# Rotation tables built by GpSimd during the networks ahead, norm sums taken in the networks' last pass, final norm and store in one block

## The chip, the cores and the metric

The kernel runs on one core of one Trainium2 chip. The metric is device time in microseconds (us): the median of several runs, and beside it one profiled execution, whose trace all rows of this text are from. PE is TensorE's matmul stream and PEld its weight loads, DVE is VectorE, ACT is ScalarE, POOL is GpSimd, SP issues DMAs. Less is better.

## What is computed

Two models in a chain over 512 real tokens and 16 meta tokens, 1024 wide, all in float32. Each feed-forward network is a norm, a gated product and a residual:

```python
def _swiglu(x, wi, wo):
    a, b = jnp.split(x @ wi, 2, axis=-1)
    return (jax.nn.silu(a) * b) @ wo
h = h + 0.5 * _swiglu(_rms_norm(h, ln), wi, wo)
```

Six of them stand around three mixers: differential attention (8 heads), sparse latent attention (16 heads, top 128 keys), and a layer of three gated branches: a state-space scan, dilated attention and memory attention. The output is `rmsnorm(h, final_norm)`. The scan is a complex linear recurrence per state:

```python
dt = exp(log_dt); mag = exp(a_re * dt); ang = a_im * dt
abar = mag * (cos(ang) + i sin(ang))
coef = (abar - 1) / (a_re + i a_im)
x_t = abar * x_{t-1} + (coef * b) u_t          # 32 groups x 64 states, 512 steps
y_t = Re(c x_t) + d u_t
```

## The kernel before

The residual stream `h` lies in SBUF, transposed: 8 chunks of 128 channels by 528 tokens. The program is a row of stages, each one or more blocks in which all engines run their own streams and meet at the end. The order is `fa_` (network 0), `a_` (differential attention), `fb_` (networks 1 and 2), `bl_` and `l_` (latent attention), `fd_` (networks 3 and 4), `s_` (scan), `d_` (heads), `g_` (merge), `ff_` (network 5), `fin_` (final norm) and `out_` (store).

**A network** (`ffn_stage`) streams its weights through two slots. ScalarE rounds them to fp32r (`wh`), VectorE takes the rest (`wl`), and TensorE multiplies three times: high by high, high by low, low by high. The upward pass has 22 chunks. The downward pass has 8, one for each chunk of `h`; VectorE adds each result to `h` (L592, semaphore `dn_h`). Where a second network follows in the same stage, ScalarE squares each finished chunk (`square`), VectorE sums the squares in `ssum` (`add_square`), and one product with a matrix of ones gives the sum over channels. After the last network of a stage nothing of this happens. GpSimd only arms the next stage's semaphores.

**A stage's norm** starts in the stage itself. ScalarE squares the even chunks and VectorE the odd ones (in `fin_` ScalarE all), TensorE adds each by a product with ones, ScalarE takes the root, VectorE the reciprocal, and then it scales eight chunks. In `a_` each scaled chunk is also split in two parts, the rest by VectorE for even chunks and by GpSimd for odd ones, and GpSimd takes the rest of the weights (`split_weights`).

**The scan stage** (`scan_stage`) turns the complex recurrence into two real ones: the inputs are rotated by minus the accumulated angle, scanned with `mag`, and rotated back. There are 16 steps (`SC`), each with 128 states. VectorE first works out dt, mag and the angle from small tiles of 128x16 (`exact_exp`, ScalarE's two sines), raises the phase by squaring nine times (`phase`), and then makes `coef`, `bbar` and `b_wide`. GpSimd waits for all phases (`phased`), builds by doubling a `fine` table of 32 angles and a `coarse` one of 16 for each state, and multiplies them out to `turns` of 512 for each step, three deep. `turns` lies in `w`, which holds u's weights, so GpSimd also waits for `u_mm`. TensorE projects u (L1878), runs 3 of 24 gate projections (L1887, `EARLY = 3`), transposes `b_wide` (L1897) and `c_wide` (L1907), makes the inputs of steps 0 and 1 (L1917), and then loops:

```python
for s in range(SC):
    for n in at_step[s]:
        gate(n)
    pe.wait_ge(scanned, 1 + s + 1)
    ...                      # y of step s (L1932), two products
    if s + 2 < SC:
        inputs(s + 2)
```

`at_step` spreads the remaining gates evenly over the steps. A gate's weights come in a ring of three and its result goes to DRAM.

**The end**: `norm_stage` writes `y_out`, and in a block of its own SP stores it in one DMA of 2 MB.

## Time and profile before

| | us |
|---|---|
| median of 3 runs (3787.04 to 3789.86) | 3788.11 |
| the profiled execution | 3787.12 |
| its span in the trace | 3785.4 |
| TensorE busy | 3596.4 (95%) |
| VectorE busy | 1742.6 (46%) |
| ScalarE busy | 1297.5 (34%) |
| GpSimd busy | 354.2 (9%) |
| scan stage, from its first square to the last y's start | 2707.2 to 3004.1 |

Busy time is time in which the profiler saw an instruction of the engine. A 512-column float32 product with 128 rows counts as two matmul instructions, which overlap, so a row's time per instruction is longer than its share. The granted clock is TensorE's, 1.00 for 2.4 GHz and 0.50 for 1.2 GHz. The trace's mean is 0.974.

### The profile page before, as it was taken

The page shows a single profiled execution, that of the slowest core. Times are in us where ns is not written, and L with a number is a line of the kernel's source. Part 1 is how long each engine was busy: PE and PEld are TensorE (multiplying, and loading weights), DVE is VectorE, ACT ScalarE, POOL GpSimd, SP SyncE. Part 2 cuts the span into 40 slices and gives each one's busy share as a digit, 9 for nine tenths or more (in the row PEclk, how much of TensorE's full clock was granted, in tenths as well). Part 3 has the DMA queues.
Part 4 walks back from the last instruction along what each step waited for, and adds up shares of the span by engine and source line. Part 5 has one row for each costly group of instructions (what it writes and reads, how often), then busy time and mean ns, then how long its engine had stood idle before and what let it go on. Part 6 is the DMA issues. An engine that isn't in the chain of part 4 may idle for free. (4 is left out here: it accounts for less than half of the span.)

```text
span 3785.4 us, 50482 instructions
## 1 busy us (share of the span) xinstructions
PE 3596.4 (95%) x20176; PEld 2938.8 (78%) x20176; DVE 1742.6 (46%) x2620; ACT 1297.5 (34%) x1784; POOL 354.2 (9%) x263
## 2 busy tenths in 40 slices
PE   8999799799999999988999999999989899899998
PEld 7999777699999999754548888888634477678886
DVE  4442366444434443276625434443358633545432
ACT  4331266443323331134524423432110144324421
POOL 0000222100000000010000000000065333320000
PEclk9999899899999999989999999999989999899999
DMA  4322311022222222300013222222212321332221
GB/s 168 138 79 87 121 51 51 17 91 91 86 84 104 89 82 84 119 28 20 1 54 109 92 91 98 100 100 84 83 50 84 113 79 55 110 113 100 100 85 70
DMA packets 115306, 318.02 MB, mean 84 GB/s; under 512 B 13335, under 2 KB 56471, under 8 KB 99060
## 3 DMA queue, kind: packets, MB, share of 16 engines
q1 hardware_dynamic: 115188, 316.48, 24.6%
q8 instruction: 70, 1.15, 0.1%
q14 instruction: 48, 0.39, 0.0%
HBM read 307.95 MB, written 17.01 MB: 86 GB/s over the span
## 5 line engine op out<-in xcount | busy, mean ns | idle before, releaser
L368 PE MATMUL acc<-fb_xh,fb_wh 128*128 128x264 f32 x1408 | 287.9, 286 | 5.7 <-DVE fb_wl L518 5.7
L368 PE MATMUL acc<-fb_xl,fb_wh 128*128 128x264 f32 x1408 | 288.3, 286 | 0.0
L368 PE MATMUL acc<-fb_xh,fb_wl 128*128 128x264 f32 x1408 | 287.9, 286 | 0.0
L368 PE MATMUL acc<-fd_xh,fd_wh 128*128 128x512 f32 x704 | 275.7, 392 | 5.7 <-DVE fd_wl L518 5.7
L368 PE MATMUL acc<-fd_xl,fd_wh 128*128 128x512 f32 x704 | 274.7, 390 | 0.0
L368 PE MATMUL acc<-fd_xh,fd_wl 128*128 128x512 f32 x704 | 274.7, 390 | 0.0
L368 PEld LDWEIGHTS acc<-fb_xh,fb_wh 128*128 128x128 f32 x1408 | 220.2, 189 | 6.0 <-DVE fb_wl L518 5.9
L439 ACT ACTIVATE fb_wh<-fb_raw 128x2048 fp32r<-128x2048 f32 (+1 forms) x74 | 124.7, 1686 | 290.1 <-PE acc L427 176.9
L368 PEld LDWEIGHTS acc<-fb_xl,fb_wh 128*128 128x128 f32 x1408 | 219.4, 189 | 0.0
L368 PEld LDWEIGHTS acc<-fb_xh,fb_wl 128*128 128x128 f32 x1408 | 219.1, 189 | 0.0
L513 DVE TENSOR_TENSOR fb_wl<-fb_raw,fb_wh 128x2048 fp32r<-128x2048 f32 (+1 forms) x74 | 148.3, 2004 | 141.3 <-ACT fb_wh L439 140.5
L439 ACT ACTIVATE fd_wh<-fd_raw 128x2048 fp32r<-128x2048 f32 (+1 forms) x74 | 124.8, 1686 | 255.8 <-PE acc L427 162.4
L513 DVE TENSOR_TENSOR fd_wl<-fd_raw,fd_wh 128x2048 fp32r<-128x2048 f32 (+1 forms) x74 | 148.3, 2004 | 136.5 <-ACT fd_wh L439 135.5
L439 ACT ACT_TABLE_LOAD x60 | 77.0, 1283 | 301.2 <-PE acc L368 301.1
L1887 PE MATMUL acc<-m_xn,s_gw 128*128 128x512 f32 x384 | 171.4, 603 | 0.0
L368 PEld LDWEIGHTS acc<-fd_xh,fd_wh 128*128 128x128 f32 x704 | 132.7, 189 | 34.5 <-DVE fd_wl L518 6.5
L368 PEld LDWEIGHTS acc<-fd_xl,fd_wh 128*128 128x128 f32 x704 | 132.6, 188 | 27.9 <-issue 0.5
L368 PEld LDWEIGHTS acc<-fd_xh,fd_wl 128*128 128x128 f32 x704 | 132.6, 188 | 27.5
L368 PE MATMUL acc<-fa_xh,fa_wh 128*128 128x264 f32 x704 | 144.7, 287 | 9.3 <-DVE fa_wl L518 9.3
L592 DVE SCALAR_TENSOR_TENSOR h<-acc,h 128x264 f32<-128x264 f32 (+1 forms) x72 | 35.2, 516 | 254.0 <-PE acc L427 254.0
L1887 PEld LDWEIGHTS acc<-m_xn,s_gw 128*128 128x128 f32 x384 | 72.6, 192 | 98.1 <-issue 98.1
L368 PE MATMUL acc<-fa_xl,fa_wh 128*128 128x264 f32 x704 | 144.7, 287 | 0.0
(541 smaller groups left out, 8653.7 us busy)
## 6 DMA issues: line engine op xcount, KB each, us to landing
fb_raw<-wi_dram SPq DMA_DIRECT2D x42, 1024.0 KB, 4.8
fd_raw<-wi_dram SPq DMA_DIRECT2D x42, 1024.0 KB, 4.8
fb_raw<-wo_dram SPq DMA_DIRECT2D x32, 704.0 KB, 4.0
fd_raw<-wo_dram SPq DMA_DIRECT2D x32, 704.0 KB, 4.0
fa_raw<-wi_dram SPq DMA_DIRECT2D x20, 1024.0 KB, 4.8
ff_raw<-wi_dram SPq DMA_DIRECT2D x20, 1024.0 KB, 4.7
a_raw<-a_qkv_dram SPq DMA_DIRECT2D x24, 512.0 KB, 4.1
s_gw<-gate_w_dram SPq DMA_DIRECT2D x24, 512.0 KB, 4.0
```

The lines of the kernel that those rows point to most:

```text
L368: last = pe.matmul(acc[:, up_base(p, b) + 2 * a + q, 0:w], x[:, k, a, :], part[:, k, t0:t0 + w], start=k == 0 and part is xh and x is wv, ...
L439: act.activation(wh[:, b, 0:n_], raw[:, b, 0:n_], ACT.Copy).then_inc(rounded, 1)
L513: dve.tensor_tensor(wl[:, b, 0:n_], raw[:, b, 0:n_], wh[:, b, 0:n_].bitcast(F32), ALU.subtract).then_inc(split, 1)
L592: last = dve.scalar_tensor_tensor(hv, acc[:, down_base(p) + 2 * (c % 2) + q, 0:w], 0.5, hv, ALU.mult, ALU.add)
L1887: last = pe.matmul(acc[:, GATE_BANK[n % 2], :], gw[:, n % 3, k * P:(k + 1) * P], xn[:, k, :], start=k == 0, stop=k == KC - 1)
```

## The change

- **Tables.** A class `RotationTables` holds `fine`, `coarse`, mag, sine and cosine. It lives from before `fd_` until after the mixer stages. In `fd_` SP loads its three inputs behind the first weight pieces (`load`), and GpSimd makes exponentials, sine and cosine (now by a series on a quarter of the angle and two doublings), the phases and both tables (`work`): some 260 instructions on 128x16 to 128x256 elements. In the scan stage VectorE's `exact_exp`, the phase squaring and ScalarE's sines are gone, `numbers()` makes `b_wide` at once, `turns` has its own memory, and GpSimd starts on the turns without a wait. `EARLY` is 0, so all 24 gates lie in the steps.
- **Norm sums.** In the last network of each stage ScalarE now squares chunks 0 to 6 in the downward pass, VectorE sums them, and a product with ones goes to a free bank with `start=True, stop=False`. The next stage squares chunk 7 alone and adds one product to the same bank. In `a_` the roundings of the first two weights move behind the root, and the lambda work on VectorE behind the scalings.
- **End.** Final norm and store share a block. SP stores two chunks at a time as they are scaled.

```diff
+                        if ahead:
+                            ahead.load(sp)
...
+                        if ahead:
+                            ahead.work(pool)
...
+                        pe.wait_ge(sq_on, 1 + (KC - 1) * len(parts) + KC - 2)
+                        for q, (t0, w) in enumerate(pieces):
+                            pe.matmul(acc[:, up_base(last_part, 1) + 2 + q, 0:w], ones[:, :], ssum[:, t0:t0 + w],
+                                      start=True, stop=False)
...
+                                elif c < KC - 1:
+                                    act.wait_ge(dn_h, 1 + 1 + KC * p + c + 1)
+                                    square(p + 1, c)
...
+                                if not more and c >= 1:
+                                    add_square(p + 1, c - 1)
...
-                        for k in range(KC):
-                            pe.wait_ge((sq_a, sq_d)[k % 2], 1 + k // 2 + 1)
-                            for b, (a, n) in enumerate(pieces):
-                                last = pe.matmul(acc[:, 2 + b, 0:n], ones[:, :], sq[:, k % 2, a:a + n],
-                                                 start=k == 0, stop=k == KC - 1)
-                            last.then_inc(nsum, 1)
+                        pe.wait_ge(sq_a, 2)
+                        for b, (a, n) in enumerate(pieces):
+                            last = pe.matmul(acc[:, 2 + b, 0:n], ones[:, :], sq[:, 0, a:a + n], start=False, stop=True)
...
-                        for k in range(0, KC, 2):
-                            if k >= 2:
-                                act.wait_ge(nsum, 1 + k - 1)
-                            act.activation(sq[:, 0, :], h[:, k, :], ACT.Square).then_inc(sq_a, 1)
-                        for c in range(2):
-                            round_weights(c)
-                        act.wait_ge(nsum, 1 + KC)
+                        act.activation(sq[:, 0, :], h[:, KC - 1, :], ACT.Square).then_inc(sq_a, 1)
+                        act.wait_ge(nsum, 2)
                         act.activation(folded(ow[:, 0, :], TOK), acc[:, 2:4, 0:wide], ACT.Sqrt,
                                        scale=1.0 / D, bias=eps_t[:, :]).then_inc(nroot, 1)
+                        round_weights(0)
                         for k in range(KC):
+                            if k == 1:
+                                round_weights(1)
...
-                    for c in range(0, KC, 2):
-                        if c >= 2:
-                            act.wait_ge(summed, 1 + c - 1)
-                        act.activation(nsq[:, 0, :], h[:, c, :], ACT.Square).then_inc(sq_a, 1)
-                    act.wait_ge(summed, 1 + KC)
-                    act.activation(folded(rstd[:, :], TOK), acc[:, 0:np_, 0:wide], ACT.Sqrt,
+                    act.activation(nsq[:, 0, :], h[:, KC - 1, :], ACT.Square).then_inc(sq_a, 1)
+                    act.wait_ge(summed, 2)
...
+        class RotationTables:
+
+
             FINE = 32
             COARSE = SEQ // FINE
+            LEVELS = (SEQ - 1).bit_length()
             ROUND = 1.5 * 2 ** 23
-            (DT, X, K, R, Q, Z, MAG, ANG, SIN, HALF, COS, NR, NI, DEN, C_RE, C_IM, T0, T1, T2, T3) = range(20)
+            (DT, LOG_DT, RE, IM, K, R, Q, ANG, MAG, SIN, COS, T0, T1) = range(13)
+            PHASE = R
+
+            def __init__(self, st):
+                self.held = sb(st, "t_fine", [P, 2, SEQ])
+                self.fine = self.held[:, :, :].rearrange("p r (s n) -> p r s n", s=SC)
+                self.coarse = sb(st, "t_coarse", [P, 2, SC, self.COARSE])
+                self.v = sb(st, "t_v", [P, 13, SC])
+                self.ki = sb(st, "t_ki", [P, SC], I32)
+                self.spare = sb(st, "t_spare", [P, SC * self.COARSE // 2])
+                self.loaded, = sems(st, "t_")
+
+            def load(self, sp):
+                sp.dma_start(self.v[:, self.RE, :], s_a[:, 0, :]).then_inc(self.loaded, 16)
+                sp.dma_start(self.v[:, self.IM, :], s_a[:, 1, :]).then_inc(self.loaded, 16)
+                sp.dma_start(self.v[:, self.LOG_DT, :], s_a[:, 2, :]).then_inc(self.loaded, 16)
+
+            def work(self, pool):
...
+                pool.wait_ge(self.loaded, 49)
+                exact_exp(DT, LOG_DT)
+                tt(RE, RE, DT, ALU.mult)
+                tt(ANG, IM, DT, ALU.mult)
+                exact_exp(MAG, RE)
+                rounded(K, ANG, 1.0 / (2 * math.pi))
+                add_times(ANG, K, -6.28125, T0)
+                add_times(ANG, K, -1.9350051879882812e-3, T0)
+                add_times(ANG, K, -(2 * math.pi - 6.28125 - 1.9350051879882812e-3), T0)
+                ts(ANG, ANG, 0.25, ALU.mult)
+                tt(T0, ANG, ANG, ALU.mult)
+                series(SIN, T0, [(-1) ** n / math.factorial(2 * n + 1) for n in range(5, -1, -1)])
+                tt(SIN, SIN, ANG, ALU.mult)
+                series(COS, T0, [(-1) ** n / math.factorial(2 * n) for n in range(6, -1, -1)])
+                for _twice in range(2):
+                    tt(T0, SIN, SIN, ALU.mult)
+                    tt(SIN, SIN, COS, ALU.mult)
+                    ts(SIN, SIN, 2.0, ALU.mult)
+                    ts(COS, T0, -2.0, ALU.mult, 1.0, ALU.add)
+
...
+                def double(table, n, room):
+                    def by(r):
+                        return v[:, PR + r, :].unsqueeze(2).to_broadcast([P, SC, n])
+
+                    t = room[:, 0:SC * n].rearrange("p (s n) -> p s n", s=SC)
+                    for r, x, y, op in ((0, 0, 1, ALU.subtract), (1, 1, 0, ALU.add)):
+                        pool.tensor_tensor(table[:, r, :, n:2 * n], table[:, 0, :, 0:n], by(x), ALU.mult)
+                        pool.tensor_tensor(t, table[:, 1, :, 0:n], by(y), ALU.mult)
+                        pool.drain()
+                        pool.tensor_tensor(table[:, r, :, n:2 * n], table[:, r, :, n:2 * n], t, op)
+                        pool.drain()
+
+                def first(table):
+                    pool.memset(table[:, 0, :, 0:1], 1.0)
+                    pool.memset(table[:, 1, :, 0:1], 0.0)
+                    pool.drain()
+
+                ts(PR, COS, 1.0, ALU.mult)
+                ts(PI, SIN, 1.0, ALU.mult)
+                unit()
+                first(self.fine)
+                room = self.coarse[:, 0, :, :].rearrange("p s n -> p (s n)")
+                for k in range(self.LEVELS):
+                    n = 1 << k
+                    if n < self.FINE:
+                        double(self.fine, n, room)
+                    else:
+                        if n == self.FINE:
+                            first(self.coarse)
+                        double(self.coarse, n // self.FINE, self.spare[:, :])
+                    if k < self.LEVELS - 1:
+                        squares()
+                        tt(RE, PR, PI, ALU.mult)
+                        tt(PR, T0, T1, ALU.subtract)
+                        ts(PI, RE, 2.0, ALU.mult)
+                        unit()
+
+        def scan_stage(st, xn, yg, tables):
...
-            EARLY = 3
+            EARLY = 0
...
-                    pool.wait_ge(phased, 2)
-                    for k in range(LEVELS):
-                        if 1 << k < FINE:
-                            double(fine, k, 1 << k)
-                        else:
-                            double(coarse, k, (1 << k) // FINE)
-                    pool.wait_ge(u_mm, 5)
-                    t = spare[:, :].rearrange("p (a b) -> p a b", a=COARSE)
+                    t = t_spare[:, :].rearrange("p (a b) -> p a b", a=COARSE)
...
-                    for c in range(KC):
-                        pe.wait_ge((sq_a, sq_d)[c % 2], 1 + c // 2 + 1)
-                        last = pe.matmul(acc[:, 4, :], ones[:, :], nsq[:, c % 2, :], start=c == 0, stop=c == KC - 1)
-                        last.then_inc(summed, 1)
+                    pe.wait_ge(sq_a, 2)
+                    pe.matmul(acc[:, 6, :], ones[:, :], nsq[:, 0, :], start=False, stop=True).then_inc(summed, 1)
...
-                    act.wait_ge(ang, 2)
-                    act.activation(v[:, SIN, :], v[:, ANG, :], ACT.Sin)
-                    act.activation(v[:, HALF, :], v[:, ANG, :], ACT.Sin, scale=0.5).then_inc(sins, 1)
...
+                    numbers()
...
         ffn_stage("fb_", 0, TOK, [(1, 2), (2, 3)], ["b_", "bl_", "l_"])
         dsa_stage()
-        ffn_stage("fd_", META, SEQ, [(3, 5), (4, 6)], ["s_"])
-        mixer_stage()
-        ffn_stage("ff_", META, SEQ, [(5, 8)], ["fin_", "out_"])
+        with ExitStack() as st:
+            tables = RotationTables(st)
+            ffn_stage("fd_", META, SEQ, [(3, 5), (4, 6)], ["s_"], ahead=tables)
+            mixer_stage(tables)
+        ffn_stage("ff_", META, SEQ, [(5, 8)], ["fin_"])
 
 
         with ExitStack() as st:
             y = sb(st, "y_out", [P, KC, SEQ])
-            norm_stage(9, "fin_", h, META, SEQ, dst=y)
-            done, = sems(st, "out_")
+            sq = sb(st, "fin_sq", [P, SEQ])
+            std = sb(st, "fin_std", [P, SEQ])
+            rstd = sb(st, "fin_rstd", [P, SEQ])
+            squared, summed, rooted, normed, done = sems(st, "fin_")
+            NORM_BANK, AT_ONCE = 2, 2
             with nc.Block() as block:
                 @block.sync
                 def _(sp):
-                    sp.dma_start(out, y[:, :, :]).then_inc(done, 16)
-                    sp.wait_ge(done, 17)
+                    for c in range(0, KC, AT_ONCE):
+                        sp.wait_ge(normed, 1 + c + AT_ONCE)
+                        sp.dma_start(out[:, c:c + AT_ONCE, :], y[:, c:c + AT_ONCE, :]).then_inc(done, 16)
+                    sp.wait_ge(done, 1 + 16 * KC // AT_ONCE)
                     sp.wait_ge(bias_there, 16 * HEADS)
                     sp.wait_ge(dil_there, 48 * SLOTS)
+
+                @block.scalar
+                def _(act):
+                    act.activation(sq[:, :], h[:, KC - 1, META:], ACT.Square).then_inc(squared, 1)
+                    act.wait_ge(summed, 2)
+                    act.activation(std[:, :], acc[:, NORM_BANK, :], ACT.Sqrt, scale=1.0 / D, bias=eps_t[:, :]
+                                   ).then_inc(rooted, 1)
+
+                @block.tensor
+                def _(pe):
+                    pe.wait_ge(squared, 2)
+                    pe.matmul(acc[:, NORM_BANK, :], ones[:, :], sq[:, :], start=False, stop=True).then_inc(summed, 1)
+
+                @block.vector
+                def _(dve):
+                    dve.wait_ge(rooted, 2)
+                    dve.reciprocal(rstd[:, :], std[:, :])
+                    dve.drain()
+                    for c in range(KC):
+                        dve.scalar_tensor_tensor(y[:, c, :], h[:, c, META:], gain[:, 9, c:c + 1], rstd[:, :],
+                                                 ALU.mult, ALU.mult).then_inc(normed, 1)
```

## Rows read from the trace of the kernel before

**Rows 1.** Windows of 100 us: PE, PEld, DVE, ACT, POOL busy us (instructions), granted clock, DMA share, GB/s

```profile
2100.00:2200.00 100.00, 100.00 (x443) 82.85 (x442) 45.32 (x47) 41.01 (x37) 0.00 (x0) 1.00 0.27 94
```

**Rows 2.** Timeline of TensorE, scan stage: start, length, line, operation, count, [idle before]

```profile
2721.09 29.83 PE L1878 MATMUL acc<-m_xn,s_w 128*128 128x512 f32 x64 [5.46 <-DVE m_xn L2022]
...
2777.35 1.97 PE L1897 MATMUL acc<-ident,s_b_wide 128*128 128x128 f32 x8 [5.83 <-DVE s_b_wide L2108]
...
2788.17 14.00 PE L1887 MATMUL acc<-m_xn,s_gw 128*128 128x512 f32 x32
2812.41 3.78 PE L1932 MATMUL acc<-s_work,s_c_t 128*128 128x512 f32 x4 [10.25 <-DVE s_work L2139]
...
2906.91 1.88 PE L1932 MATMUL acc<-s_work,s_c_t 128*128 128x512 f32 x4
...
2917.60 1.88 PE L1932 MATMUL acc<-s_work,s_c_t 128*128 128x512 f32 x4
...
2935.16 1.88 PE L1932 MATMUL acc<-s_work,s_c_t 128*128 128x512 f32 x4
...
3004.06 1.88 PE L1932 MATMUL acc<-s_work,s_c_t 128*128 128x512 f32 x4
```

**Rows 3.** Timeline of VectorE, scan stage: scalings, and the first instruction of steps 0 and 1

```profile
2720.19 5.39 DVE L2022 SCALAR_TENSOR_TENSOR m_xn<-h,gain,s_spare 128x512 f32<-128x512 f32 x8 [0.46 <-issue]
...
2801.80 0.69 DVE L2117 TENSOR_TENSOR s_work<-acc,s_w 128x512 f32<-128x512 f32 x1 [24.51 <-POOL s_w L1860]
...
2812.52 0.69 DVE L2117 TENSOR_TENSOR s_work<-acc,s_w 128x512 f32<-128x512 f32 x1 [0.16 <-issue]
```

**Rows 4.** Window from the first y on, columns as in rows 1

```profile
2812.40:2824.00 11.60, 11.59 (x13) 4.19 (x14) 10.85 (x16) 0.00 (x0) 10.57 (x11) 0.50 0.01 1
```

**Rows 5.** Timeline of ScalarE, start of the scan stage

```profile
2707.23 0.63 ACT L1943 ACTIVATE s_work<-h 128x512 f32<-128x512 f32 x1 [14.57 <-PEq L319]
...
2713.41 1.28 ACT L1945 ACT_TABLE_LOAD   x1
2715.66 0.69 ACT L1945 ACTIVATE s_spare<-acc,eps_t 128x512 f32<-128x512 f32 x1 [0.97 <-PE acc L1871]
```

**Rows 6.** Tiles, squares of three norms: count, ns min/median/max, first and last start

```profile
L979 ACT ACTIVATE a_sq<-h x4: 642/643/643, 414.3 to 419.9; 128x528 f32<-128x528 f32 x4
...
L1337 ACT ACTIVATE b_nsq<-h x4: 642/643/643, 1560.0 to 1567.3; 128x528 f32<-128x528 f32 x4
...
L225 ACT ACTIVATE fin_sq<-h x8: 612/630/631, 3760.7 to 3767.0; 128x512 f32<-128x512 f32 x8
```

**Rows 7.** Timelines of ScalarE: the roots of the same three norms

```profile
423.80 0.70 ACT L983 ACTIVATE a_ow<-acc,eps_t 128x528 f32<-128x528 f32 x1
...
1570.17 0.70 ACT L1339 ACTIVATE b_rstd<-acc,eps_t 128x528 f32<-128x528 f32 x1 [0.97 <-PE acc L1270]
...
3768.99 0.69 ACT L227 ACTIVATE fin_std<-acc,eps_t 128x512 f32<-128x512 f32 x1
```

**Rows 8.** Timelines of GpSimd and VectorE, head stage, while both subtract

```profile
3013.98 2.35 POOL L2282 TENSOR_TENSOR d_wl<-d_raw,d_wh 128x1024 fp32r<-128x1024 f32 x1 [47.95 <-ACT d_wh L2464]
...
3020.20 2.86 DVE L2661 TENSOR_TENSOR d_xl<-m_xn,d_xh 128x512 fp32r<-128x512 f32 x1
```

**Rows 9.** Timeline of GpSimd, scan stage: first doublings, first turn

```profile
2770.73 0.27 POOL L1831 TENSOR_TENSOR s_fine<-s_fine,s_phase 128x16 f32<-128x16 f32 x1 [62.28 <-DVEq L2059]
...
2771.72 0.23 POOL L1831 TENSOR_TENSOR s_fine<-s_fine,s_phase 128x16 f32<-128x16 f32 x1
...
2794.61 1.05 POOL L1857 TENSOR_TENSOR s_w<-s_coarse,s_fine 128x512 f32<-128x512 f32 x1
...
2796.80 1.26 POOL L1860 TENSOR_TENSOR s_w<-s_w,s_spare 128x512 f32<-128x512 f32 x1
```

**Rows 10.** Tiles y_out and gate_scratch: us from a DMA's issue to its landing

```profile
DMA to landing us min/median/max: 6.2/6.2/6.2
...
DMA to landing us min/median/max: 2.0/4.0/11.1
```

297 lines of the change are left out of this document (109 added, 188 removed).

## The prediction, made before the changed kernel was seen

> **What bounds the kernel now.** I read the busy time by stretches of 100 us first. In the feed-forward networks TensorE is busy the whole stretch, while VectorE and ScalarE have half or more of their time free [rows 1] (the stretches from 2000 to 2700 are alike in it). So nothing that the change puts on those two, or on GpSimd, inside a network costs time unless TensorE comes to wait for it. What can be won lies where TensorE stands still: at the four norms that follow a network (fa_, fb_, fd_, ff_) and inside the scan stage.
>
> Next came TensorE's order of work in the scan stage [rows 2]. It projects u in 29.7 us from 2721.09 (the row's 29.83 less the last product's tail), runs three gates, stands 5.8 us before the transposes of b_wide, which VectorE brought late, does 10.8 us of transposes and first inputs (2777.35 to 2788.17), runs two gates, and stands 10.3 us before y of step 0. VectorE's rows say why: step 0 could start only when GpSimd's turn tables came, after 24.5 us of waiting [rows 3]. From then on VectorE needs 10.72 us a step. TensorE's steps take 10.69 us with one gate and 17.56 us with two [rows 2], so a gate is 6.87 us and TensorE sets the pace from there. The first step after the gap is slow: y takes 3.78 us in place of 1.88, and the granted clock is 0.50 of full speed for the 11.6 us from there, the 1.2 GHz level, after ten microseconds without work [rows 2, 4]. The norm ahead of u takes from ScalarE's first square at 2707.23 to the root at 2715.66 [rows 5], and then VectorE's reciprocal and eight scalings of 0.67 us stand before TensorE [rows 3].
>
> **The change part by part.** *The scan's middle.* After the change the tables are there when the stage starts, the b_wide chain is short, and all 24 gates lie in the 16 steps (two and one by turns). Counted with this trace's own rows: u 29.7, transposes and first inputs 10.8, then eight steps of 17.56 and eight of 10.69, less 5.6 because the last two steps have no inputs behind them and I stop at the start of the last y: 220.4. Sum 260.9. Before, from 2721.09 to 3004.06 it was 283.0. **Gain 22.1 us**: the 5.8, the 10.3, and about 6 of half-speed steps. A pair of steps takes TensorE 28.2 us and VectorE 21.4, so TensorE never waits in the loop. The new b_wide chain (some 30 small operations of VectorE, 7 us, and 3.7 us for c_wide) lies under u's 29.7 us. If that cover were gone each microsecond would count in full; I find about 8 us of slack even with the blocking below. The stage's tail (last y, gelu) is unchanged.
>
> *The scan's norm.* One square (0.63 us), then the table load (1.28 us) and the root [rows 5]: the root starts at 2707.23 + 0.63 + 1.28 = about 2709.2 in place of 2715.66, 6.5 us earlier. The product of u's weights has by then landed or is just about to. But GpSimd now makes its first three turns at once from the stage's start: 18 instructions of 1.05 to 1.26 us that read SBUF twice [rows 9], in the very time in which VectorE scales xn, also with two SBUF inputs. Later in this trace two such streams meet: VectorE's subtraction of 512 elements, 0.69 us for this shape [rows 3], takes 2.86 us beside GpSimd's of 2.35 [rows 8], its own work plus the whole of the other. So I take one GpSimd instruction (1.1 us) ahead of each scaling: eight take 8 x 1.75 = 14.0 us, u's first quarter ends about 15.2 us after the first scaling starts. Unblocked it would be 0.9 + 9.2 (29.83 less three quarters of 6.87) = 10.1. **Cost 5.0** (ends: 0, and 8 when the longest instruction stands ahead each time and TensorE stays at 1.2 GHz a little longer). **Net gain 1.4.**
>
> These sentences can be left out. The Trainium skill, page "SBUF — State Buffer", section "SBUF: two separate sides", says that VectorE and GpSimd share one pair of SBUF ports as an exclusive lock held for a whole instruction, against VectorE's instructions with two SBUF inputs when GpSimd's reads SBUF. By that rule the scan's steps, which read PSUM, say nothing on the norm's scalings; the sum is the one I took, and without the lock it would be 5.0 us lower here. The trace agrees at the 2.86 us row.
>
> *The norm before differential attention.* First square at 414.3, so the root starts at 414.3 + 0.64 + 1.28 = 416.2 instead of 423.80 [rows 6, 7]: 7.6 us. GpSimd's first two weight subtractions (2.35 us each, the shape of [rows 8]) lay under the reciprocal and now fall among the scalings and on GpSimd's own share of x: one whole subtraction and a bit, cost 2.5 (0 to 4.7). **Gain 5.1.** The lambda work moved behind the scalings is under 1 us and ends before ScalarE asks for it.
>
> *The norm before the latents.* GpSimd idles. First square 1560.0, root at 1562.0 instead of 1570.17 [rows 6, 7]: 8.2. The four squares span 7.3 us from first to last here and 5.6 in the attention's norm [rows 6], 1.7 more for the same work, and part of that may stay: I take **7.8** (6.6 to 8.2). The chain behind it is TensorE's own, so the gain passes on.
>
> *The final norm and the store.* Root at 3760.7 + 0.63 + 1.28 = 3762.6 in place of 3768.99 [rows 6, 7]: 6.4. The store of 2 MB lands 6.2 us after its issue, one of 256 KB in 2.0 at best [rows 10]; the line through both gives 2.6 for the last 512 KB, and the three ahead of it go out while VectorE scales (two scalings, 1.3 us, against 1.2 us of transfer). Ends 2.0 and 6.2. **Gain 6.4 + 3.6 = 10.0.**
>
> *What is added.* In a network's last pass seven squares on ScalarE and six additions on VectorE lie under TensorE's down products, which have no gap [rows 1]; if they had no cover they would cost 0.7 us each. At its end one sum product follows the last down product: 6.87/8 = 0.86 us, beside VectorE's last update of 0.69, so 0.25 for each of four networks (0 to 0.86). **Cost 1.0.** In fd_ three small loads go into SP's queue behind six weight pieces and ahead of loads that wait for splits anyway: nothing. GpSimd's table work is some 260 instructions. The small ones take 0.23 to 0.27 us and start 0.33 apart [rows 9]; I take 0.4, since nearly each is drained, for 206 of them. The other 54 are the doublings, which took 24 us in the scan stage (2770.73 to 2794.61). Together 106 us; the operation with a constant isn't in the trace, bounded by 0.23 and by 1.26 us, the shortest and longest of [rows 9], and 260 of the longest make 330 us. Both lie inside the 707 us from 2000 to the stage's start, in which the network keeps TensorE busy [rows 1, 5]. They hold up VectorE's two-input work by up to 0.23 us each. In the steady chunks that is under slack; in the network's first 15 us about ten such holds, 2.5 us, fall on the chain of squares and splits, part of which TensorE waits for. No row here tells how much; nearer to the lower end, since TensorE starts the first chunk before the loads have landed that GpSimd waits for: **cost 0.7** (0 to 2.5).
>
> Sum: 22.1 + 1.4 + 5.1 + 7.8 + 10.0 - 1.0 - 0.7 = 44.7 us. The profiled execution took 3787.12 us around its span of 3785.4, so 3742.4; the median of the runs is 1.0 above it: **3743.4 us**.
>
> **The rivals.** (1) *No holding up.* GpSimd's turns run beside VectorE's steps all through the loop and the steps stay at 10.72 us [rows 3]; if the norms' scalings are as free, 5.0 and 2.5 come back: 3735.9. Against it stands the 2.86 us row. Chance 0.15. (2) *The clock stays low into the loop.* The transposes are short and broken by ScalarE's copies; should the clock fall there as it fell at the gap, the 11.6 us of TensorE's work run at 1.2 GHz [rows 4] cost about 6 us again: 3749.4. Against it: TensorE has no gap of several microseconds any more. Chance 0.17. (3) *The middle gives nothing*, because something I didn't see holds the first step (u's copies, a gate's weights): norms and store alone, 44.7 - 22.1 = 22.6: 3765.5. Chance 0.05. (4) *Slower: the tables aren't done when fd_ ends.* GpSimd has over 707 us for 260 instructions, 2.7 us each; the block's end waits for it beyond that. With 44.7 us won elsewhere it decides from (707 + 44.7)/260 = 2.9 us an instruction; at 3.2 us (832 in all) the kernel takes 3788.1 - 44.7 + 125 = 3868. The slowest row is 1.26 us [rows 9]. Chance 0.01.
>
> **The numbers.** The forecast itself has 0.62, with its own range 3738 to 3749 from the bounds of the norms' blocking, the store and the network ends. The range for 8 in 10 reaches to rivals 1 and 2: 3734 to 3752. A measurement of this kernel tells about 0.2%, 7.6 us, from no change. All cases but the last are faster by more; unseen mishaps that eat 37 us get 0.02: faster 0.97, same 0.02, slower 0.01.
>
> **What would show it.** In the new profile: TensorE from the start of u to the last y in about 266 us (260.9 plus the 5.0 of held-up scalings) with no gap of 5 us; VectorE's xn scalings in the scan 1.6 to 2 us apart in place of 0.67 (right) or 0.67 (rival 1); GpSimd done with the tables about 110 to 180 us into fd_; the first gates after the transposes at full clock, or at 0.5 (rival 2); each root 6.4 to 8.2 us nearer to the stage's first square; the last store landing some 3 us after the last scaling. The prediction fails if TensorE waits in the loop, if TensorE's clock stays low through u, or if fd_'s chunks stretch beyond their present length.

## The result, and the profile after

The changed kernel takes **3735.9 us** (median of 4 runs, 3735.22 to 3740.57) against 3788.2 for the kernel before in the same session (4 runs, 3787.04 to 3789.86): ratio 0.9868, 95% interval 0.9852 to 0.9883, 52.3 us faster. 3743.4 was forecast, 7.5 us more; the time lies in the wide range (3734 to 3752) and below the forecast's own (3738 to 3749). The two spans differ by 50.7 us, the prediction's sum was 44.7: 6 us came from somewhere else.

The page of the kernel after, its span and part 1:

```profile
span 3734.7 us, 50566 instructions
PE 3566.8 (96%) x20104; PEld 2920.9 (78%) x20104; DVE 1741.1 (47%) x2492; ACT 1300.1 (35%) x1793; POOL 440.0 (12%) x465
```

Where the 50.7 us came from is read by stages: the same TensorE instruction is looked up in both traces, and the stretch between two such marks compared. The last column gives the same stretch in all the traces of this study whose code is the same there as in the kernel after (n of them).

| stretch | before | after | gain | forecast | same code as after |
|---|---|---|---|---|---|
| start to fa_'s last product | 412.9 | 412.0 | 0.9 | 0 | 411.8 to 413.1 (10) |
| to fb_'s first product (attention) | 369.6 | 364.7 | 4.8 | 5.1 | 362.4 to 366.1 (7) |
| fb_'s last product to the first product of xn (latents' norm) | 16.74 | 8.59 | 8.15 | 7.8 | 8.59 (10) |
| rest of the latent stages, to fd_'s first product | 408.9 | 406.7 | 2.2 | 0 | 406.5 to 410.2 (10) |
| fd_, first to last product | 721.6 | 721.7 | -0.1 | -0.7 | 721.5 to 722.6 (8) |
| to u's first product (scan's norm) | 15.28 | 9.46 | 5.8 | 6.4 | 9.4 to 9.6 (6) |
| u | 29.83 | 31.52 | -1.7 | -5.0 | 31.4 to 31.6 (6) |
| end of u to the last y | 253.1 | 229.1 | 24.1 | 22.1 | 229.1 (9) |
| heads and merge | 385.8 | 389.1 | -3.3 | 0 | 387.4 to 389.2 (11) |
| ff_'s last product to the end | 26.18 | 16.05 | 10.1 | 10.0 | 16.03 to 16.06 (8) |

fb_ and ff_ with their starts make up the small rest (-0.2). In four of the ten traces with the new norm sums fd_ takes 722.2 to 722.6 us and in the others 721.5 to 721.7: TensorE's granted clock rose to 1.00 only 5.2 to 6.0 us after fd_'s first product in those four, 3.7 to 4.1 after it in the rest. norms_alone, which has no tables in fd_, is one of the four. The forecast's network ends (-1.0) lie inside the norms' rows: from a network's last product to the norm's own takes 0.06 to 0.12 us more than before, 0.35 for all four.

TensorE in the scan stage, which answers to [rows 2]:

```profile
2699.48 6.34 PE L1944 MATMUL acc<-m_xn,s_w 128*128 128x512 f32 x10 [6.13 <-DMA s_w<-s_u_dram]
...
2709.27 21.73 PE L1944 MATMUL acc<-m_xn,s_w 128*128 128x512 f32 x50 [0.55 <-DVE m_xn L2082]
2730.83 1.04 PE L1963 MATMUL acc<-ident,s_b_wide 128*128 128x128 f32 x8
2731.77 1.06 PE L1973 MATMUL acc<-ident,s_work 128*128 128x128 f32 x8
2733.47 1.15 PE L1973 MATMUL acc<-ident,s_work 128*128 128x128 f32 x8 [0.63 <-ACT s_c_t L2027]
...
2737.24 2.74 PE L1983 MATMUL acc<-s_u_t,s_b_t 32*128 32x512 f32 x8
2739.90 14.00 PE L1953 MATMUL acc<-m_xn,s_gw 128*128 128x512 f32 x32
2753.74 1.88 PE L1998 MATMUL acc<-s_work,s_c_t 128*128 128x512 f32 x4
...
2764.43 1.88 PE L1998 MATMUL acc<-s_work,s_c_t 128*128 128x512 f32 x4
...
2781.99 1.88 PE L1998 MATMUL acc<-s_work,s_c_t 128*128 128x512 f32 x4
```

No gap longer than 0.63 us is left between u and the loop, the first y takes 1.88 us, and steps are 10.69 and 17.56 us apart. Two things are new: u waited for its **weights** (the releaser is a DMA), not for xn, and from the first transpose to the first gate 9.07 us pass, where the prediction put 10.8. VectorE in the same stage, and then ScalarE, answering to [rows 3, 5]:

```profile
2697.64 11.57 DVE L2082 SCALAR_TENSOR_TENSOR m_xn<-h,gain,s_spare 128x512 f32<-128x512 f32 x8
...
2739.31 0.69 DVE L2104 TENSOR_TENSOR s_work<-acc,s_turns 128x512 f32<-128x512 f32 x1 [15.10 <-issue]
```

```profile
2691.54 0.63 ACT L2006 ACTIVATE s_work<-h 128x512 f32<-128x512 f32 x1 [14.16 <-PEq L279]
2692.18 1.28 ACT L2008 ACT_TABLE_LOAD   x1
2693.48 0.69 ACT L2008 ACTIVATE s_spare<-acc,eps_t 128x512 f32<-128x512 f32 x1
```

Square to root: 1.94 us for 8.43. The eight scalings take 11.57 us where they took 5.39: held up, but by less than the 14.0 of the prediction. GpSimd's rows beside them show both sides waiting; alone these three shapes take 1.05, 1.05 and 1.26:

```profile
2699.67 1.29 POOL L1925 TENSOR_TENSOR s_turns<-t_coarse,t_fine 128x512 f32<-128x512 f32 x1 [0.16 <-issue]
2700.93 1.49 POOL L1926 TENSOR_TENSOR s_t_spare<-t_coarse,t_fine 128x512 f32<-128x512 f32 x1
2702.56 1.53 POOL L1928 TENSOR_TENSOR s_turns<-s_turns,s_t_spare 128x512 f32<-128x512 f32 x1
```

The windows (columns as in rows 1): GpSimd's tables in fd_, and the first step's clock, which is full where [rows 4] had 0.50:

```profile
2000.00:2100.00 100.00, 100.00 (x442) 82.78 (x442) 45.39 (x45) 41.01 (x37) 72.96 (x194) 1.00 0.27 98
...
2753.00:2765.00 12.00, 12.00 (x29) 4.97 (x28) 11.30 (x17) 0.97 (x2) 7.85 (x8) 1.00 0.24 66
```

GpSimd's last table instruction ended at 2112.1, 144 us after fd_'s first product and 138.5 after its own first; 106 had been counted, 110 to 180 expected. The final norm's root and the landing of the four stores, answering to [rows 7, 10]:

```profile
3722.09 0.69 ACT L2914 ACTIVATE fin_std<-acc,eps_t 128x512 f32<-128x512 f32 x1
```

```profile
DMA to landing us min/median/max: 2.6/2.6/2.6
```

### The profile page after: what moved, and what is told of

Its sections match the earlier page's. It is cut to its first block and busy times, and to the rows that moved or that the text cites. A ratio compares the mean times of both kernels' runs of the same rounds, so it can differ in the third digit from the quotient of the medians.

```text
span 3734.7 us, 50566 instructions
## 1 busy us (share of the span) xinstructions
PE 3566.8 (96%) x20104; PEld 2920.9 (78%) x20104; DVE 1741.1 (47%) x2492; ACT 1300.1 (35%) x1793; POOL 440.0 (12%) x465
## 5 line engine op out<-in xcount | busy, mean ns | idle before, releaser
L689 POOL TENSOR_TENSOR a_wl<-a_raw,a_wh 128x1024 fp32r<-128x1024 f32 x32 | 76.0, 2376 | 661.0 <-ACT a_wh L885 661.0
```

Source lines behind the costliest of these rows:

```text
L689: pool.tensor_tensor(wl[:, c % RING, :], raw[:, c % RING, :], wh[:, c % RING, :].bitcast(F32), ALU.subtract).then_inc(split, 1)
```

## The experiments

The kernel before had medians of 3786.3 to 3789.2 us in the sessions of this study. So between variants timed in different sessions a difference of some 3 us is read from the stages of their traces, one for each variant, and not from the medians.

### One half of the change at a time: norms_alone

```diff
 # the kernel before, with the change in ffn_stage, the four norms and the final block
+                                elif c < KC - 1:
+                                    act.wait_ge(dn_h, 1 + 1 + KC * p + c + 1)
+                                    square(p + 1, c)
...
+                        pe.wait_ge(sq_on, 1 + (KC - 1) * len(parts) + KC - 2)
```

> The kernel before with the norms' part alone: squares summed beside the networks' last chunks, the four norms with one square each, the final norm and its four stores in one block. The scan stage keeps its own tables, early gates and table work of GpSimd. By the prediction's terms: attention 5.1, latents 7.8, scan's norm 6.5 with nothing held up by GpSimd's turns, final norm and store 10.0, network ends -1.0: 28.4 us faster than before, 3759 to 3760 us. Theory A (the extra 6 to 7.6 us of the whole change came with the norms' part): 33 to 36 us faster, about 3753. Theory B (it came with the scan's middle): 28 us faster or a little less, since the product of u's weights now waits for their landing, about 6 us after the root, and so only 5.9 of the 6.5 us can be had.

Measured: 3760.1 us (3759.35 to 3760.75, 5 runs; before 3789.2 in the same session), ratio 0.9922 (0.9909 to 0.9936): 29.1 us faster, 28.4 by the terms. Theory B held, A fell: the extra did not come with the norms. Here too u waits 6.14 us for its weights, so the scan's norm gives 5.8 of its 6.5 us.

### The other half: tables_alone

```diff
 # after, with those same hunks undone: eight squares per norm, norm_stage, one store
-                    act.activation(nsq[:, 0, :], h[:, KC - 1, META:], ACT.Square).then_inc(sq_a, 1)
-                    act.wait_ge(summed, 2)
+                    for c in range(0, KC, 2):
+                        if c >= 2:
+                            act.wait_ge(summed, 1 + c - 1)
+                        act.activation(nsq[:, 0, :], h[:, c, META:], ACT.Square).then_inc(sq_a, 1)
+                    act.wait_ge(summed, 1 + KC)
```

> The kernel after with the norms' part undone: old norms (eight squares each), old final norm and one store, but the rotation tables made beside fd_, no early gates, turns from the stage's start. By the prediction's terms: 22.1 for the scan's middle, less 5.0 for scalings held up by the turns, less 0.7 at fd_'s start: 16.4 us faster than before, 3771 to 3772 us. Theory B (the middle is worth more because the transposes and first inputs run at the full clock and the held-up scalings hide behind the landing of u's weights or cost less than 5): 22 to 26 us faster, 3762 to 3766. The interval from the start of u to the last y: 266 by the prediction, 260 to 262 by theory B.

Measured: 3769.3 us (3768.58 to 3771.28, 5 runs), ratio 0.9948 (0.9934 to 0.9962): 19.9 us, between the prediction's 16.4 and theory B's 22 to 26. In the trace theory B is right on its own ground: from u's start to the last y 261.3 us (283.0 before, 266 forecast). The weights had landed before the first scaling here, so this trace shows what held-up scalings cost by themselves:

```profile
2720.33 11.36 DVE L2140 SCALAR_TENSOR_TENSOR m_xn<-h,gain,s_spare 128x512 f32<-128x512 f32 x8 [0.46 <-issue]
```

```profile
2721.23 5.61 PE L1995 MATMUL acc<-m_xn,s_w 128*128 128x512 f32 x8 [5.46 <-DVE m_xn L2140]
2727.17 1.12 PE L1995 MATMUL acc<-m_xn,s_w 128*128 128x512 f32 x2 [0.33 <-DVE m_xn L2140]
2728.84 1.12 PE L1995 MATMUL acc<-m_xn,s_w 128*128 128x512 f32 x2 [0.55 <-DVE m_xn L2140]
...
2731.75 21.73 PE L1995 MATMUL acc<-m_xn,s_w 128*128 128x512 f32 x50 [0.33 <-DVE m_xn L2140]
```

u takes 32.24 us where it took 29.83: **2.4 us**, not 5.0. In this kernel the turns also held up two of VectorE's four squares ahead of the root (0.88 and 1.24 us for 0.69), and the root came 0.74 us later after fd_'s last product than in the kernel before. The kernel after has no square on VectorE there.

### turns_late

```diff
+                    pool.wait_ge(normed, 1 + KC)
                     for s in range(SC):
```

> The kernel after, but GpSimd begins its turns only when all eight scalings of xn are done. If two-input work of GpSimd is what stretches the scalings from 0.67 us apart to 1.45, they are 0.67 apart here and all eight take 5.4 us in place of 11.6. What TensorE wins by it: theory 1 (the prediction's cost of 5.0 for held-up scalings is right in size): 4 to 5 us. Theory 2 (TensorE waits for the landing of u's weights until 2 us after the first scaling starts, and runs through its first quarter at half clock beside the scalings, so that the hold-up costs only what the waits inside the first quarter sum to): 1 to 1.5 us, 3734.5 in place of 3735.9. The interval from the start of u to its last product 30.2 in place of 31.4 us. The turns end about 11 us later, at about 2727 on the scale of after, still before step 0 at 2739, so nothing is lost there.

```profile
2699.75 5.39 DVE L2083 SCALAR_TENSOR_TENSOR m_xn<-h,gain,s_spare 128x512 f32<-128x512 f32 x8
```

```profile
2701.51 29.83 PE L1945 MATMUL acc<-m_xn,s_w 128*128 128x512 f32 x64 [6.05 <-DMA s_w<-s_u_dram]
```

Without GpSimd beside them the scalings take 5.39 us again: its turns were the cause of the 11.57. From the first scaling to u's end 31.6 us pass, 33.4 in after; 1.8 us came back in the stage, as theory 2 said. The whole took 3735.9 (3734.97 to 3736.13, 4 runs), no better than after: in its trace fd_ and the latent stages were together 2.5 us longer than in after's, which the edit doesn't touch.

### u_quarters

```diff
-                    sp.dma_start(w[:, :, :], s_u.rearrange("c p n -> p c n")).then_inc(u_there, 16)
+                    for c in range(4):
+                        sp.dma_start(w[:, c, :], s_u[c]).then_inc(quarter[c], 16)
...
+                    pool.wait_ge(normed, 1 + KC)
...
-                    pe.wait_ge(u_there, 17)
                     for c in range(4):
+                        pe.wait_ge(quarter[c], 17)
```

> The kernel after with GpSimd's turns begun after the scalings (as in the run turns_late) and u's weights in four loads of 512 KB, each with a semaphore of its own, in place of one of 2 MB that landed 7.9 us after its issue. In turns_late TensorE started 1.76 us after the first scaling because of that landing. Theory (held-up scalings and the landing cover each other, and only with both gone does the cost come back): the first quarter lands 4 us after its issue, TensorE starts 0.9 us after the first scaling, from the first scaling's start to u's end 30.7 us in place of 33.4 in after and 31.6 in turns_late: 2.6 us faster than after, 3733.3. Rival (the four loads share the queue so that the first quarter lands hardly earlier): 31.6, 3734.2.

```profile
2697.70 29.82 PE L1947 MATMUL acc<-m_xn,s_w 128*128 128x512 f32 x64 [5.19 <-DVE m_xn L2085]
```

The first quarter landed 3.2 us after its issue, and TensorE waits for xn again. First scaling to u's end: 30.7 us, 2.65 less than in after, as forecast. 3733.3 us (3731.16 to 3736.84, 4 runs) against 3733.3 expected; with that spread the equal digits are luck, and the trace's 2.65 us are the evidence. So both covers were real: the landing hid 0.9 of the norm's gain, and while it did, it hid a part of the hold-up.

### one_store

```diff
-            NORM_BANK, AT_ONCE = 2, 2
+            NORM_BANK, AT_ONCE = 2, KC
```

> The kernel after, but one store of 2 MB once all eight scalings are done, in the same block, in place of four of 512 KB. If the four stores bring what the landing times say: the store lands 6.2 us after its issue in place of 2.6, so 3.6 us slower than after, 3739.5, and the rest of the final norm is unchanged. If the joining of the two blocks brought part of the 3.6 (rival), less than that.

The one store lands 6.2 us after its issue, and from ff_'s last product to the end 19.66 us pass in place of 16.05: 3.6, all of it the store's. 3740.4 us (3738.81 to 3743.11, 4 runs).

### tables_4x

```diff
                 pool.wait_ge(self.loaded, 49)
+                ts(13, RE, 1.0, ALU.mult)          # RE kept in a slot of its own
+                for _again in range(4):          # the whole table work is in this loop
```

> The kernel after with GpSimd's table work done four times over before the last result stands: about 1,050 small instructions in place of 263, 134 us each time by the trace of after, so about 537 us, still inside the 718 us of fd_. The prediction's theory (it lies under TensorE's products; it holds VectorE up only in the network's first microseconds): no change, 3735.9 within 1, and TensorE from fd_'s first product to its last is as long as in after within 0.3 us. Rival (each small instruction costs fd_ something that TensorE sees in the steady chunks too): at 0.02 us of TensorE's time each, 16 us slower.

```profile
1968.00:2108.00 140.00, 139.23 (x605) 114.80 (x606) 75.46 (x77) 65.21 (x67) 98.88 (x253) 0.98 0.30 108
2108.00:2500.00 392.00, 392.00 (x1729) 324.30 (x1728) 169.46 (x164) 141.49 (x133) 285.82 (x764) 1.00 0.27 96
```

GpSimd works until 2514 and TensorE is busy in all of the 392 us of the second window; fd_ takes 721.5 us, and the kernel 3736.6 (3735.77 to 3737.29, 4 runs). Table work costs nothing in this network as long as it ends inside, even fourfold: rival 4 had no ground up to there.

### b_wide_late

```diff
                     dve.memset(b_wide[:, :, :, :], 0.0)
+                    dve.wait_ge(u_mm, 5)
                     numbers()
```

> The kernel after, but VectorE begins the chain to b_wide only when u's last product is done, so TensorE stands still ahead of the transposes, as it did before the change. b_wide was ready 10.5 us ahead of u's end in after; its chain takes 11 us from the last scaling, so TensorE now waits 9 to 12 us. Theory (the prediction took 10.8 us for the transposes and first inputs from a stretch that ran at 1.2 GHz after a gap; without the gap they take 9.1): here they take 10.8 again, so the loss is the wait plus 1.7 us, and the time from the first gate to the last y stays 220.2 or grows by the steps at half clock, 2 us at most. Sum 11 to 14 us slower than after, 3747 to 3750. Rival (9.1 is due to something else, the order of inputs and gates): 9.1 again, and the loss is the wait alone.

```profile
2735.93 1.97 PE L1963 MATMUL acc<-ident,s_b_wide 128*128 128x128 f32 x8 [6.24 <-DVE s_b_wide L2076]
2739.59 3.37 PE L1973 MATMUL acc<-ident,s_work 128*128 128x128 f32 x16 [1.69 <-DVE s_work L2093]
2743.20 1.14 PE L1973 MATMUL acc<-ident,s_work 128*128 128x128 f32 x8 [0.24 <-ACT s_c_t L2027]
```

The wait was 6.2 us and not 9 to 12 (VectorE's chain is shorter than I took it), so the loss is 9.7 us in the stage: 6.4 ahead of the transposes, and 3.3 from the first transpose to the first gate (12.36 us for 9.07). Of these 3.3, 1.1 are further waits, since c_wide came late too. The kernel took 3745.1 (3744.35 to 3745.76, 4 runs). After the gap the eight b transposes take 1.97 us, as in [rows 2], where they take 1.04 in after, and transposes and first inputs take 10.2 us besides their waits, 8.0 in after. The clock is the reason that the windows show, from the first transpose to the first gate in the kernel before, in after and in b_wide_late (columns as in rows 1):

```profile
2777.35:2788.17 10.82, 10.68 (x49) 7.98 (x49) 0.00 (x0) 5.59 (x9) 8.67 (x23) 0.72 0.00 1
...
2730.83:2739.90 9.07, 8.04 (x49) 5.41 (x47) 0.59 (x1) 7.14 (x11) 0.00 (x0) 1.00 0.00 0
...
2735.93:2748.29 12.36, 10.23 (x49) 7.26 (x49) 4.13 (x10) 6.76 (x10) 0.00 (x0) 0.74 0.00 0
```

From the first gate on, nothing differs: 220.15 us both times. The half-speed cost is local to the first microseconds behind the gap.

### before_again

The kernel before, unchanged, profiled once more.

> The kernel before, unchanged, profiled once more. It tells how much of a stage's length is chance. In the traces so far the heads and output stages together (from the last y of the scan to the last product of the merge) took 385.8 us before, and 3.3, 3.0 and 2.8 us more in the changed kernel and in the two halves of the change, none of which touches them; the latents' and their heads' stages behind the norm took 2.0 us less in the changed kernel. If this is chance of TensorE's clock periods, this trace differs from the first one by 1 to 3 us in such stages, and the stages inside the networks by less than 0.3. If the heads stage is 385.8 again within 0.5, the change made it 3 us longer.

Its span is 3789.5 us, 4.1 more than the first trace's, with the same program. Heads and merge took 387.6, so 1.8 of the 3.3 us that this stretch "lost" was one lucky trace. 2.3 us more than in the first trace lie in the attention stage, where the reciprocal came late (VectorE, then GpSimd):

```profile
424.11 1.65 DVE L1110 TENSOR_TENSOR a_lam_pr<-a_lam_in 128x128 f32<-128x128 f32 x1 [3.09 <-DMA a_g_sub<-a_subln_dram]
425.68 0.14 DVE L1111 TENSOR_SCALAR a_g_qk<-a_g_qk 128x1 f32<-128x1 f32 x1
...
426.16 3.44 DVE L1116 RECIPROCAL a_ow<-a_ow 128x528 f32<-128x528 f32 x1
```

```profile
420.95 4.66 POOL L716 TENSOR_TENSOR a_wl<-a_raw,a_wh 128x1024 fp32r<-128x1024 f32 x2 [418.13 <-ACT a_wh L914]
```

The root ended at 423.83. VectorE stood ahead of the reciprocal in a wait for three small loads of the lambda work. They came at 424.11, the small product behind them took 1.65 us in place of 0.29, and the reciprocal began 2.3 us late. The loads themselves were only 0.3 us behind the root. The product has both inputs in SBUF, and it ended at 425.76, just behind GpSimd's second weight subtraction (from 423.26 to 425.61). In tables_alone it was the same (2.18 us, ended at 426.12, GpSimd's at 425.98). In the first trace of before the loads had come by 423.83, 0.1 us ahead of the start of that subtraction, and the product took 0.29. So the three traces fit a slightly late load whose delay GpSimd's instruction lengthened; no run took the subtraction away to test it.

Whether the kernel loses the 2.3 us is open. tables_alone had the same delay, and its whole attention stretch took 369.2 us against 369.6 in the first trace of before and 371.9 in this one; TensorE was busy for 311.2 us in it, for 314.0 and 313.9 in those two.

### lambda_moved

```diff
 # the kernel before; the group goes behind the eight scalings
-                        dve.wait_ge(c_in, 49)
-                        dve.tensor_tensor(lam_pr[:, :, :], lam_in[:, 0:4:2, :], lam_in[:, 1:4:2, :], ALU.mult)
...
                         dve.wait_ge(nroot, 2)
```

> The kernel before with one line group moved: VectorE's lambda work of the attention stage, with its wait for three small loads, stands behind the eight scalings in place of ahead of the reciprocal. In the first trace of before the loads had landed when the root was ready and the reciprocal began at its end (11.65 us after the network's last product); in before_again and tables_alone, with the same code, the loads landed at the root's end, the small product behind them took 1.65 us in place of 0.29, and the reciprocal began 2.3 us late (13.95). Theory (the wait ahead of the reciprocal costs 0 or 2.3 us by the luck of the loads, the work itself nothing): the reciprocal begins 11.6 to 11.7 us after the network's last product here, whatever the loads do, and the median lies 0 to 2.3 us under before's. Rival (the 2.3 us come from the squares or the root being late in those runs): 13.95 appears here too.

The reciprocal began 11.65 us after fa_'s last product, right behind the root. The time, 3786.0 us against 3788.05 (11 and 15 runs), ratio 0.9997 (0.9988 to 1.0006), is too near to tell. One trace can't show that 13.95 never comes here; that nothing stands before the reciprocal any more can be read in the code. The attention stretch took 369.2 us, as in tables_alone with the late reciprocal.

### split_late and attention_x

```diff
 # split_late: GpSimd's second weight piece behind its four pieces of x
-                        for c in range(2):
-                            split_weights(c)
+                        split_weights(0)
 # attention_x: besides, four buffers of x, and all eight rests of x on VectorE
-                            pool.tensor_tensor(xl[:, k, :], lg[:, 0, 1, :], xh[:, k, :].bitcast(F32),
-                                               ALU.subtract).then_inc(x_lo_p, 1)
+                                dve.tensor_tensor(xl[:, k, :], lg[:, k % 4 // 2, k % 2, :],
+                                                  xh[:, k, :].bitcast(F32), ALU.subtract).then_inc(x_lo_d, 1)
```

attention_x also puts ScalarE's second weight rounding behind its eight roundings of x.

> The kernel after, but in the attention stage GpSimd subtracts its second piece of weights after its four subtractions of x, in place of ahead of them. In after that piece took 2.60 us from 423.45 and VectorE's two scalings beside it took 3.53 us in all; from the reciprocal to ScalarE's first square of a projection 27.65 us passed (26.6 to 26.8 in three other kernels with the same code), 24.6, 24.5 and 23.4 in those that have the old norm, where both pieces lay ahead of the scalings. Theory (the hold-up measured at 2.3 to 3.1 us, forecast 2.5, comes from these two pieces, and the second has most of it because it delays x's second chunk too): about 1.9 us back: 24.9 to 25.7 us, the kernel 1.9 us faster, 3734.0. Rival (the chain of VectorE, ScalarE and GpSimd over two buffers sets the pace whatever GpSimd does first): 26.6 or more, 3735.9. TensorE's low clock comes and goes by 1 to 2 us in this stage from run to run, so the interval is read from the trace.

> The kernel after, but in the attention stage x is split without GpSimd: four buffers of normed x in place of two, all eight subtractions on VectorE, and GpSimd subtracts weights only ahead of and behind x. In after a pair of chunks takes 3.3 us: VectorE's 0.69 x 2 + 0.71 and GpSimd's 1.3 during which VectorE stands. Theory (GpSimd's instruction holds VectorE's two-input work for its whole length, so VectorE alone is faster than both): a pair takes 4 x 0.71 = 2.9 us, and the second weight piece no longer blocks: from the reciprocal to ScalarE's first square 22.5 to 23.5 us in place of 26.6 to 27.7, the kernel 4 us faster, 3732. Rival (two engines side by side are worth their sharing): 3.3 us a pair or more, no gain beyond the 1.9 of the moved weight piece.

VectorE in this stage, first in after, then in attention_x:

```profile
419.69 2.07 DVE L1080 SCALAR_TENSOR_TENSOR a_lg<-h,gain,a_ow 128x528 f32<-128x528 f32 x1
422.46 0.71 DVE L1084 TENSOR_TENSOR a_xl<-a_lg,a_xh 128x528 fp32r<-128x528 f32 x1 [0.71 <-ACT a_xh L956]
423.08 3.53 DVE L1080 SCALAR_TENSOR_TENSOR a_lg<-h,gain,a_ow 128x528 f32<-128x528 f32 x2
```

```profile
424.72 0.76 DVE L1075 SCALAR_TENSOR_TENSOR a_lg<-h,gain,a_ow 128x528 f32<-128x528 f32 x1
425.40 0.70 DVE L1080 TENSOR_TENSOR a_xl<-a_lg,a_xh 128x528 fp32r<-128x528 f32 x1
426.02 0.76 DVE L1075 SCALAR_TENSOR_TENSOR a_lg<-h,gain,a_ow 128x528 f32<-128x528 f32 x1
```

In after a scaling beside GpSimd's first weight piece takes 2.07 us, two beside the second 3.53. From the reciprocal's start to ScalarE's first square of a projection: 27.65 us in after, 25.2 in split_late (3733.5 us, 3732.95 to 3735.53), and 20.2 in attention_x (3732.1 us, 3731.55 to 3732.77; 4 runs each). A pair of chunks takes VectorE alone 2.6 us, the two engines together 3.3. split_late came out as its theory said. attention_x gained more than expected (22.5 to 23.5), but it changed two things at once. In after VectorE stands 0.71 us before each of its rests, waiting for ScalarE's rounding over two buffers (the row at 422.46 above); with four buffers that wait is gone, and 0.7 us is the whole difference between 3.3 and 2.6. Four buffers with the rests still shared were not tried, so what GpSimd's share costs by itself isn't shown. The kernel's median is 3.8 us under that of after (1.9 when each is taken against the kernel before of its own session). The trace has 8.1 in this stage, and 3.2 of them went in longer latent stages (410.0 us), whose code is the same.

### best

attention_x and u_quarters together, and the last 512 KB of the store as two pieces.

> The kernel after with three things together: x of the attention stage split on VectorE alone (attention_x), turns begun behind the scalings with u's weights in four loads (u_quarters), and the last 512 KB of the final store as two of 256 KB. By the terms: 4 + 2.6 + 0.6 = 7.2 us faster than after, 3728.7 us. If the two stages' gains are there in the trace but TensorE's clock periods take some of it back, 3729 to 3732.

3726.7 us (3725.56 to 3730.07, 5 runs; before 3786.3 in the same session), ratio 0.9841 (0.9828 to 0.9855). The median is 9.2 us under that of the kernel after, and no run of the one reaches a run of the other, though they were timed in different sessions and the two intervals still overlap (0.9852 to 0.9855). The trace bears the two stages out: reciprocal to first square 19.8 us, first scaling to u's end 30.6. The latent stages took 410.2 us, as in attention_x (410.0); the eight other traces with that code have 406.5 to 408.6. So the longer latent stages may belong to attention_x's edit, and what makes them longer stays open. The finer store gave nothing: each piece of 256 KB lands after 2.6 us, like one of 512, and from ff_'s last product to the end it is 16.03 for 16.05.

## Why the prediction was right, and where its sizes were off

**The scan's middle** (22.1, measured 24.1): right in mechanism. Both gaps went, the tables were there, TensorE paced every pair of steps (28.25 us for 28.2). The mis-sized term is "10.8 us of transposes and first inputs": that stretch stood behind a gap of 5.8 us, and its granted clock was 0.72 in the mean (0.50 for its first 6 us). Without the gap it is 9.07 at 1.00, though 1.03 us of waits came in, and b_wide_late brings the slow transposes back. With the 220.15 from the first gate to the last y (220.4 in the sum) this gives the 2 us. b_wide was ready 10.4 us before u ended, 8 had been found.

**The scan's norm** (net 1.4, measured 4.1): the root came 6.5 us sooner after the stage's first square (1.94 for 8.43), as forecast. "One GpSimd instruction ahead of each scaling", 1.75 us each, was the right picture with too high a price: 1.45 each, 11.4 to 11.6 us for eight in place of 14.0. The rows it was taken from had the lower price too. [rows 8] show two instructions that did not run together: beside VectorE's 2.86 us, which began at 3020.20, GpSimd's subtraction began at 3019.69 and took 2.82, and the next one began 2.8 us after it. So the pair took 2.8 us and not 0.69 + 2.35 = 3.04. The hold-up cost 2.4 us where nothing else was late (tables_alone), 1.7 in after. The weights, said to have "by then landed or just about to", landed 1.8 us after the first scaling had begun; that took 0.9 us of the gain and hid part of the hold-up. By the exclusive lock that the Trainium skill states (page "SBUF — State Buffer", section "SBUF: two separate sides") three turns' instructions and three scalings would need, by my estimate from their times alone, 3.36 + 2.0 = 5.4 us; the rows show 4.6 for such a group (from GpSimd's instruction at 2699.67 to the one at 2704.23). The trace and turns_late agree that one engine holds the other up; they don't agree that the whole length of each instruction is added.

**The norm before attention** (5.1, measured 4.8 in the first pair of traces): the root came 7.6 us sooner after the stage's first square, as forecast, and from the reciprocal to the first square of a projection it took 2.0 to 3.3 us longer (26.6 to 27.8 in the seven traces with this code) than in the two profiles of before (24.6 and 24.5; the cost forecast was 2.5). "The lambda work is under 1 us" was true of the work; the wait ahead of it could delay the reciprocal by 2.3 us, and the change took that out too. What that is worth to the kernel isn't shown. Over all traces the stretch is 369.2 to 371.9 us with the old norm (3) and 362.4 to 366.1 with the new.

**The latents' norm** (7.8, measured 8.15), **the final norm and store** (10.0, measured 10.1, of which 3.6 is the store's, shown by one_store), **the network ends** (-1.0, measured -0.35) and **fd_'s start** (-0.7, measured nothing): right, the small costs taken too high. The added squares and GpSimd's tables don't show in TensorE's time. Beside the tables VectorE's largest subtraction takes 2.292 us on average, 2.293 before, and its small operations on average at most 0.04 more.

**The rivals.** 3735.9 is to the digit what rival 1 gave, and it was wrong: the scalings were held up. Its number came about because other terms were too low. So it is partly luck that the wide range holds the time: its lower end was set by this rival, which did not happen. Rival 2 (low clock into the loop) didn't happen, the clock is 1.00 there; rivals 3 and 4 neither.

**The sum.** Of the 6 us between spans, 2.0 are the middle, 2.7 the scan's norm and u, 1.4 network ends and fd_'s start, and all the rest sums to nearly nothing, though in it stages that the change doesn't touch are up to 3.3 us longer or 2.2 shorter. Those may be chance, as the repeats scatter as widely (last column of the table). But for the heads and merge the traces of before, before_again and lambda_moved have 385.8 to 387.9 and the eleven changed ones 387.4 to 389.2, with means 1.4 us apart, so that a cost of about that size there stays open.

## What to carry to other kernels

Before a duration from a trace goes into a sum, look at the clock of its stretch: a row behind a gap can be a half-speed row, and once the gap goes it shortens too. When a norm or any head of a stage is made shorter, ask what arrives next: here u's weights, one load of 2 MB that became the thing waited for and wanted cutting in four. GpSimd took a long chain of small work beside a network free of charge here, but at a stage's head its two-input work is better begun when VectorE is through, and a wait for a small load should not stand ahead of a critical instruction in the same queue.

## What the runs showed of the hardware

Eight scalings of VectorE took 5.39 us alone and 11.4 to 11.6 beside GpSimd's two-input work, each engine's instructions lengthened (GpSimd's from 1.05, 1.05 and 1.26 us to 1.29, 1.49 and 1.53). Eight 128x128 transposes took 1.97 us at a granted clock of 0.50 behind a gap and 1.04 us at 1.00. A store of 256 KB from this kernel's end landed no sooner than one of 512 KB (2.6 us both), though [rows 10] have one of 256 KB at 2.0. One program's spans differed by 4.1 us between two profiles, with 2.3 of it in the attention stage.
